# First norm of a two-layer transformer kernel: row sums on TensorE, four units tile by tile, bias tables moved

## The chip, the cores and the metric

The kernel runs on one core of one Trainium2 chip. The metric is device time in microseconds (us), the median of three runs. Engine names are those of the profile: PE is TensorE, DVE is VectorE, ACT is ScalarE, POOL is GpSimd, SP issues the DMAs.

## The reference

The kernel computes two hybrid transformer layers on x (512 positions by 1024). Each sublayer first normalizes: `adaln_pre(h, g, shift, scale) = rms_norm(h, g) * (1 + scale) + shift`, where shift and scale are products of `ada_w` (1024 by 9216 per layer) with `silu(c)`. The first sublayer is a gated feed-forward network:

```
def swiglu(h, w13, w2):
    a, b = jnp.split(h @ w13, 2, axis=-1)
    return (jax.nn.silu(a) * b) @ w2
```

Attention, short convolution, gated delta rule and mLSTM follow, then a second feed-forward sublayer. Everything is float32. Attention adds a bias that depends on the distance of two positions (`t5_table[t5_bucket(dist)]`); the kernel builds these bias tables once.

## The kernel before

Activations are kept transposed: tile k of 8 holds 128 of the 1024 channels for all 512 positions. Every float32 operand of the large products is split in a high part (an ACT copy to fp32r) and a low part (a DVE subtraction), and each product takes three fp32r matmuls: high by high, low by high, high by low. Each engine has a queue that runs in program order, and semaphores join them. All the work that the change touches lies in the first 100 us, in the first feed-forward sublayer of layer 0:

- **Start.** SP loads the constants, x, the condition `cond`, the tables of the bias, and 8 parts of `ada_first` of 1 MB each (L1117 to L1128), with the weights of units 0 and 1 between them. PE turns x into 8 banks (L3413), ACT copies them to `xT` (L1755) and squares them (L1761), PE sums the squares against ones (L3430). DVE makes the shift and scale: 16 dot products along rows of 1024 (`first`, L1985; `dots`, L1982), then one addition and one scaling for all 8 tiles (`prepare_start`, L2852). PE runs fillers (`warm`, L3674) until that is done.
- **Norm.** For each of two halves of the positions and each k, DVE writes `hf` (L2292), ACT the high part `hH` (L1527), DVE the low part `hL` (L2298).
- **Units.** A unit is 128 output columns of `w13`: 8 tiles, three matmuls each. Units 0 and 1 go half by half as `hL` comes, unit 2 behind them (`open_three`, L3461 to L3463); unit 3 runs last, whole (`products_third`, L3482 to L3484).
- **Bias tables.** PE forms distance rows by one-hot products (L3418 to L3421), ACT copies them out (L1770 to L1773), SP writes them to DRAM and reads them back skewed (`SKEW`, `CSKEW`, L1184, L1185). Between units 2 and 3 PE flips the skewed rows (L3440) and ACT copies them to `bm` (L1781). POOL copies `cb` out of `CSKEW` (L3305) once the last `hL` is written, and then makes four sums `tF` (L3324).
- **First pair.** After unit 3, `chunk` begins with `classical(f, 0)` (L3539 to L3541), 48 matmuls, whose weights come from `RW`: ACT splits the first 8 tiles (`group1`, L1357), DVE makes their low part (L2057). `pair_out` on DVE (L2176, L2178) needs ACT's Silu of unit 0 and its copy `pair_high` (L1458).

## Time and profile before

| what | us |
|---|---|
| median of three runs | 3389.28 (3389.25 to 3390.62) |
| the profiled execution | 3389.15 |
| its span in the profile | 3387.4 |
| first matmul of unit 0 | 44.11 |
| first matmul of the first pair | 70.48 |

The span covers the program's instructions; 1.75 us of the execution lie around it. Engine times in the trace are counted from the start of the span. Times of PE are modelled at their end, so that starts are compared.

### The profile page before, as it was taken

What the parts mean: (1) busy time and instruction counts of PE and PEld (TensorE: products, weight loads), DVE (VectorE), ACT (ScalarE), POOL (GpSimd) and SP (SyncE); (2) the same over time, 40 slices, a digit from 0 to 9 for tenths busy, and PEclk for the clock granted to TensorE, in tenths of its full rate; (3) what the DMA queues carried; (4) which work ended last, traced back from release to release, by engine and by line L of the source; (5) the groups of instructions that cost most, each with busy time, mean ns of one, the idle gap of its engine ahead of it and who ended that gap; (6) DMA issues with size and microseconds to landing.
All of it is one profiled execution on the core that took longest, in us unless ns stands there. A gap on an engine that the chain in (4) does not pass through costs nothing. (4 is left out here: it accounts for less than half of the span.)

```text
span 3387.4 us, 51035 instructions
## 1 busy us (share of the span) xinstructions
PE 3329.7 (98%) x19808; PEld 2811.7 (83%) x19808; DVE 2267.5 (67%) x3615; ACT 1317.6 (39%) x2095; POOL 438.0 (13%) x329
## 2 busy tenths in 40 slices
PE   8999999999999999999999999999999999999999
PEld 7989877788888898987778888886888888788887
DVE  6877757658775677785765877657666525766642
ACT  5424344535333433334453523243443324443321
POOL 2000200222000300020022200121200011120002
PEclk9999999999999999999999999999999999999999
DMA  6463523113542345442201353321233332223332
GB/s 252 148 229 129 166 86 94 32 39 127 176 145 96 112 154 211 144 150 88 87 26 54 128 192 124 101 77 52 81 99 99 105 102 63 68 82 94 96 104 85
DMA packets 88629, 380.90 MB, mean 112 GB/s; under 512 B 9774, under 2 KB 10926, under 8 KB 77192
## 3 DMA queue, kind: packets, MB, share of 16 engines
q1 hardware_dynamic: 88456, 378.52, 33.5%
q8 instruction: 117, 1.92, 0.2%
q14 instruction: 56, 0.46, 0.0%
HBM read 376.36 MB, written 2.12 MB: 112 GB/s over the span
## 5 line engine op out<-in xcount | busy, mean ns | idle before, releaser
L2001 DVE TENSOR_TENSOR wL<-wR,wH 128x1024 fp32r<-128x1024 f32 (+2 forms) x160 | 207.9, 1299 | 195.4 <-ACT wH L1289 195.2
L1289 ACT ACTIVATE wH<-wR 128x1024 fp32r<-128x1024 f32 (+2 forms) x158 | 175.0, 1107 | 381.3 <-PE bank L3452 305.6
L3697 PE MATMUL bank<-hH,wH 128*128 128x512 f32 x640 | 271.6, 424 | 0.0
L3566 PE MATMUL bank<-gHc,wH 128*128 128x512 f32 x660 | 256.8, 389 | 0.0
L3567 PE MATMUL bank<-gHc,wL 128*128 128x512 f32 x660 | 256.8, 389 | 0.0
L3568 PE MATMUL bank<-gLc,wH 128*128 128x512 f32 x660 | 256.7, 389 | 0.0
L3699 PE MATMUL bank<-hL,wH 128*128 128x512 f32 x640 | 251.6, 393 | 0.0
L3539 PE MATMUL bank<-hH,wH 128*128 128x512 f32 x640 | 249.7, 390 | 1.2 <-DVE wL L2057 1.2
L3698 PE MATMUL bank<-hH,wL 128*128 128x512 f32 x640 | 250.5, 391 | 0.0
L3540 PE MATMUL bank<-hH,wL 128*128 128x512 f32 x640 | 249.4, 390 | 0.0
L3541 PE MATMUL bank<-hL,wH 128*128 128x512 f32 x640 | 249.0, 389 | 0.0
L3450 PE MATMUL bank<-hH,wH 128*128 128x512 f32 x640 | 249.0, 389 | 0.0
L3451 PE MATMUL bank<-hH,wL 128*128 128x512 f32 x640 | 249.0, 389 | 0.0
L3452 PE MATMUL bank<-hL,wH 128*128 128x512 f32 x640 | 249.0, 389 | 0.0
L3149 DVE SCALAR_TENSOR_TENSOR xn<-bank,par,xn 128x511 f32<-128x511 f32 (+1 forms) x176 | 131.6, 747 | 120.3 <-ACT xn L1921 108.6
L1982 DVE CUSTOM_DVE_ANT_0 adaw<-adaw,cond 128x1024 f32<-128x1024 f32 x144 | 194.6, 1370 | 10.7 <-DMA adaw<-in_ada_w 10.3
L2057 DVE TENSOR_TENSOR wL<-RW,wH 128x512 fp32r<-128x512 f32 (+1 forms) x200 | 189.7, 977 | 15.1 <-ACT wH L1361 7.9
L3493 PE MATMUL bank<-tH,wH 128*128 128x256 f32 x640 | 181.1, 283 | 0.0
L3494 PE MATMUL bank<-tH,wL 128*128 128x256 f32 x640 | 181.1, 283 | 0.0
L3495 PE MATMUL bank<-tL,wH 128*128 128x256 f32 x640 | 181.1, 283 | 0.0
L1389 ACT ACTIVATE wH<-wR 128x1408 fp32r<-128x1408 f32 x52 | 71.8, 1381 | 261.7 <-PE bank L3568 261.7
L3697 PEld LDWEIGHTS bank<-hH,wH 128*128 128x128 f32 x640 | 121.0, 189 | 40.0 <-issue 19.6
(567 smaller groups left out, 8683.0 us busy)
## 6 DMA issues: line engine op xcount, KB each, us to landing
RW<-in_ffn_wq SPq DMA_DIRECT2D x80, 1024.0 KB, 5.6
adaw<-in_ada_w SPq DMA_DIRECT2D x144, 512.0 KB, 4.4
wR<-in_w_up SPq DMA_DIRECT2D x88, 512.0 KB, 3.6
wR<-in_ffn_w SPq DMA_DIRECT2D x56, 704.0 KB, 4.1
wR<-in_w_mix SPq DMA_DIRECT2D x72, 512.0 KB, 3.6
wR<-in_w_down SPq DMA_DIRECT2D x32, 704.0 KB, 4.1
wR<-in_w_in SPq DMA_DIRECT2D x40, 512.0 KB, 3.6
ada<-in_ada_first SPq DMA_DIRECT2D x8, 1024.0 KB, 12.1
```

The source lines that it names most:

```text
L3450: pe.matmul(o, wH[n][:, k, :], rH[:, r, :], start=start and k == 0, stop=False)
L3451: pe.matmul(o, wL[n][:, k, :], rH[:, r, :], start=False, stop=False)
L3452: mm = pe.matmul(o, wH[n][:, k, :], rL[:, r, :], start=False, stop=stop and k == tiles - 1)
L3539: pe.matmul(o, wh[:, k, :], hH[:, r, :], start=start and k == 0, stop=False)
L3540: pe.matmul(o, wl[:, k, :], hH[:, r, :], start=False, stop=False)
L3541: mm = pe.matmul(o, wh[:, k, :], hL[:, r, :], start=False, stop=not start and k == TT - 1)
L3566: pe.matmul(o, wh[:, k, :], gHc[:, k, c], start=k == 0, stop=False)
L3567: pe.matmul(o, wl[:, k, :], gHc[:, k, c], start=False, stop=False)
L3568: mm = pe.matmul(o, wh[:, k, :], gLc[:, k, c], start=False, stop=k == KH - 1)
L3697: pe.matmul(o, wH[n][:, k, :], hH[:, k, :], start=k == 0, stop=False)
L3698: pe.matmul(o, wL[n][:, k, :], hH[:, k, :], start=False, stop=False)
L3699: mm = pe.matmul(o, wH[n][:, k, :], hL[:, k, :], start=False, stop=k == KT - 1)
```

## The change

SP's order is new: `par` comes ahead of the parts, unit 3's load and the parts 5 to 7 follow by their waits, and the bias rows' write and the skewed reads stand behind the first pair's load and ahead of the second's. DVE moves four of the eight tiles of x and adds up the squares; PE sums them with one matmul instead of sixteen. For five of eight tiles the dot products go to PE: `part_sums` multiplies 8 row blocks, four at a time on 32 columns each, with the turned condition, ACT copies the sums, `part_columns` adds the four groups (a weight load of 128 columns for one output column). DVE keeps the last three as before. Shift, scale and norm then go tile by tile over all positions, and so do the four units (`first_four`). The fillers are gone. The bias rows are formed inside `first_four`, and the flips stand right ahead of the first pair, which waits for all four copies. `ada_first` is laid out by column for the five parts, on the host. Left out below: the tiles' places, semaphore names, the small helpers of ACT and DVE that the text names.

```diff
-ADA_PARTS = tuple((2 * c, 2 * c + 2) for c in range(KT))
+FIRST_TILES = (26, 30, 34, 38, 8, 12)
+FIRST_PE = 5
...
-        ada0 = [place(f"ada0{j}", [P, KT, D], at=at) for j, at in enumerate((o_g + 28 * TB, o_h))]
+        first_rows = [place(f"ada0{t}", [P, 2, D], at=o_g + t * TB) for t in FIRST_TILES]
+        ada0 = [first_rows[c] for c in (0, 1, 2, 3, 4, 0, 1, 5)]
...
+            sp.dma_start(par[:, 0:C_END1], a["par1"][0]).then_inc(S.par_in, 16)
...
-                ada_part(c)
-                if c < 2:
-                    sp.dma_start(wR[c][:, 0:KT, :], a["ffn1_w13"][0, c]).then_inc(S.w_in[c], 16)
+                if c in (5, 6):
...
+                if f == 0 and l == 0:
+                    for k in range(2):
+                        ada_part(k)
+                        sp.dma_start(wR[k][:, 0:KT, :], w13[l, k]).then_inc(S.w_in[k], 16)
+                    for k in range(2, 5):
+                        ada_part(k)
+                    unit(ubase + 2, w13[l, 2], KT, 0)
+                    ada_part(5)
+                    unit(ubase + 3, w13[l, 3], KT, 1)
+                    for k in range(6, KT):
+                        ada_part(k)
+                    sp.wait_ge(S.dc, 4)
...
+                    sp.wait_ge(S.dc, 4)
+                    pair(f, 0, wq, l)
                     sp.wait_ge(S.bias_sb, 1)
                     sp.dma_start(bias_dram, BROW[:, :]).then_inc(S.bias_out, 16)
                     sp.dma_start(cbias_dram, CROW[:, :]).then_inc(S.bias_out, 16)
-                unit(ubase + 2, w13[l, 2], KT, 0)
-                if start:
-                    sp.wait_ge(S.ada0_done, 4)
-                elif f:
-                    sp.wait_ge(S.c_o, at(S.c_o, TT))
-                pair(f, 0, wq, l)
-                unit(ubase + 3, w13[l, 3], KT, 1)
-                if start:
                     sp.wait_ge(S.bias_out, 32)
-                    sp.wait_ge(S.x_turned, KT)
+                    sp.wait_ge(S.dc, 5)
+                    sp.wait_ge(S.ada0_done, 2)
                     sp.dma_start(SKEW[:, :, :], bass.AP(bias_dram.tensor, 0, [[1, P], [640, H], [1, T]])).then_inc(S.skew_in, 16)
                     sp.dma_start(CSKEW[:, :, :], bass.AP(cbias_dram.tensor, 0, [[1, P], [1056, H], [1, 896]])).then_inc(S.skew_in, 16)
-                pair(f, 1, wq, l)
+                    pair(f, 1, wq, l)
...
-                gate_silu(0, 0)
-                pair_high(0)
                 if between:
                     between()
-                gate_silu(1, 2)
-                group1(f, 0)
-                single(f, 0, 2, 2)
-                sum_high(f, sub, 0)
-                pair_high(1)
-                act.wait_ge(S.w_used, at(S.w_used, ubase + 4))
-                single(f, 0, 3, 5)
-                if between:
+                    gate_silu(0, 0)
+                    group1(f, 0)
+                    pair_high(0)
+                    gate_silu(1, 2)
+                    act.wait_ge(S.w_used, at(S.w_used, ubase + 4))
+                    single(f, 0, 2, 2)
+                    single(f, 0, 3, 5)
+                    pair_high(1)
+                    sum_high(f, sub, 0)
                     act.wait_ge(S.cb_set, 1)
...
+            def first_norm():
+                for j in range(TT):
+                    k = 2 * j + 1
+                    act.wait_ge(S.x_turned, k + 1)
+                    act.activation(xT[:, k, :], bank[k][:, :], ACT.Copy).then_inc(S.x_copied, 1)
+                    first_square(2 * j)
+                    first_square(2 * j + 1)
+                act.wait_ge(S.ct, 1)
+                act.activation(CT[:, :, :], bank[4][:, 0:2 * P].rearrange("p (k c) -> p k c", k=KT), ACT.Copy).then_inc(S.ct, 1)
+                first_high(0)
+                first_sums(0)
+                first_high(1)
+                first_sums(1)
+                act.wait_ge(S.ms, 1)
+                act.activation(rstd[:, :], bank[MS_BANK[0]][:, :], ACT.Ln, bias=eps, scale=1.0 / D).then_inc(S.ln, 2)
+                logs[0] += 2
+                act.wait_ge(S.ln, 2)
+                act.activation(rstd[:, :], rstd[:, :], ACT.Exp, scale=-0.5).then_inc(S.rstd, 2)
+                first_sums(2)
+                for k in range(KT):
+                    for e, c in enumerate(HALVES):
+                        act.wait_ge(S.hf, 2 * k + e + 1)
+                        act.activation(hH[:, k, c], HB[e][k // TT][:, k % TT, :], ACT.Identity,
+                                       bias=mod[:, k:k + 1]).then_inc(S.h_hi, 1)
+                    if k == 0:
+                        first_sums(3)
+                        first_high(2)
+                    if k == 1:
+                        first_sums(4)
+                    if k == 2:
+                        first_high(3, fourth)
+                    if k == 3:
+                        first_bias()
...
+                def normed(k):
+                    if k == 0:
+                        dve.wait_ge(S.x_copied, TT)
+                        dve.wait_ge(S.rstd, 2)
+                    dve.wait_ge(S.mod0, 2 * k + 2)
+                    for e, c in enumerate(HALVES):
+                        dve.scalar_tensor_tensor(HB[e][k // TT][:, k % TT, :], xT[:, k, c], modA[:, k:k + 1], rstd[:, c],
+                                                 ALU.mult, ALU.mult).then_inc(S.hf, 1)
+                def normed_low(k):
+                    for e, c in enumerate(HALVES):
+                        dve.wait_ge(S.h_hi, 2 * k + e + 1)
+                        dve.scalar_tensor_tensor(hL[:, k, c], HB[e][k // TT][:, k % TT, :], mod[:, k:k + 1],
+                                                 hH[:, k, c].bitcast(F32), ALU.add, ALU.subtract).then_inc(S.h_lo, 1)
+                def part(c):
+                    if c >= FIRST_PE:
+                        first(c)
+                    shifted(c)
+                    scaled_by(c)
                 begin(0)
-                for c in range(KT - 1):
-                    first(c)
-                    if 0 < c < 3:
-                        lo_seam(0, c - 1)
+                for k in range(0, KT, 2):
+                    dve.wait_ge(S.x_turned, k + 1)
+                    dve.tensor_copy(xT[:, k, :], bank[k][:, :]).then_inc(S.x_moved, 1)
+                for k in range(1, KT):
+                    if k < KT - 1:
+                        dve.wait_ge(S.sq0, k + 1)
+                    else:
+                        dve.wait_ge(S.last_sq, 2)
+                    if k > 1:
+                        dve.wait_ge(S.sq_sum, k - 1)
+                    dve.tensor_tensor(squares[0], squares[0], squares[k], ALU.add).then_inc(S.sq_sum, 1)
                 dve.wait_ge(S.par_in, 16)
-                first(KT - 1)
-                dve.wait_ge(S.ada0_done, KT)
-                dve.tensor_tensor(mod[:, 0:2 * KT], mod[:, NMOD:NMOD + 2 * KT], col(C_ADAB, 2 * KT), ALU.add).then_inc(S.mod_set, 1)
-                dve.wait_ge(S.mod_set, at(S.mod_set, 1))
-                dve.scalar_tensor_tensor(modA[:, 0:KT], mod[:, KT:2 * KT], 1.0, col(C_NORM, KT), ALU.add,
-                                         ALU.mult).then_inc(S.mod_set, 1)
-                dve.wait_ge(S.mod_set, at(S.mod_set, 2))
+                low(0)
+                part(0)
+                low(1)
+                part(1)
+                normed(0)
+                normed(1)
+                for k in range(KT):
+                    normed_low(k)
+                    if k + 2 < KT:
+                        part(k + 2)
+                        normed(k + 2)
+                    if k in (1, 3):
+                        low(2 + k // 2)
+                dve.tensor_tensor(shd[:, :], mod[:, TT:KT], mod[:, 0:TT], ALU.subtract).then_inc(S.t_d, 1)
+                dve.sem_inc(S.mod_set, 2)
...
+                for r in range(2):
+                    for g in range(4):
+                        mm = pe.matmul(bank[DS_BANK[c % 2]][32 * g:32 * (g + 1), 0:2 * P], CT[:, 4 * r + g, :], rows[:, 4 * r + g, :],
+                                       start=r == 0, stop=r == 1)
+                mm.then_inc(S.ds, 1)
...
+            def part_columns(c):
+                if c == 0:
+                    pe.wait_ge(S.picks, 2)
+                if c >= 2:
+                    pe.wait_ge(S.mod0, 2 * c - 3)
+                pe.wait_ge(S.ds, 2 * c + 2)
+                for j in range(2):
+                    mm = pe.matmul(bank[DC_BANK[c % 2]][:, j:j + 1], DS[c % 2][:, j * P:(j + 1) * P], picks[:, :], start=True, stop=True)
+                mm.then_inc(S.dc, 1)
+            part_sums(0)
+            pe.wait_ge(S.sq_sum, KT - 1)
+            pe.matmul(bank[MS_BANK[0]][:, :], ones, squares[0], start=True, stop=True).then_inc(S.ms, 2)
+            part_columns(0)
+            part_sums(1)
+            part_columns(1)
+            part_sums(2)
...
+            def bias_rows():
+                pe.wait_ge(S.tab_in, 64)
+                pe.wait_ge(S.dc, FIRST_PE)
+                pe.wait_ge(S.mod0, 2 * FIRST_PE)
+                pe.matmul(bank[3][0:H, :], tab[:, :], OHR[:, 0:512], start=True, stop=True)
+                pe.matmul(bank[5][0:H, 256:384], tab[:, :], OHR[:, 512:640], start=True, stop=True)
+                for b, c, w, o in ((4, 0, 512, 0), (7, 512, 512, 0), (5, 1024, 32, 384)):
+                    mm = pe.matmul(bank[b][0:H, o:o + w], tab[:, :], OHF[:, c:c + w], start=True, stop=True)
+                mm.then_inc(S.bias_ps, 1)
...
+            def first_four():
...
+                pe.wait_ge(S.w_lo, 2)
+                for k in range(KT):
+                    pe.wait_ge(S.h_lo, 2 * k + 2)
+                    for u in range(2):
+                        part(u, k)
+                    if k < 3:
+                        part_columns(k + 2)
+                    if k < 2:
+                        part_sums(k + 3)
+                    if k == 2:
+                        bias_rows()
+                        pe.wait_ge(S.w_lo, 3)
+                        for r in range(2):
+                            part(2, r)
+                    if k >= 2:
+                        part(2, k)
+                    if k == 4:
+                        pe.wait_ge(S.w_lo, 4)
+                        pe.wait_ge(S.bias_sb, 1)
+                        for r in range(4):
+                            part(3, r)
+                for k in range(4, KT):
+                    part(3, k)
...
                 else:
+                    if between:
+                        between()
+                        pe.wait_ge(S.bm_set, H)
                     classical(f, 0)
...
-                open_three(ubase, n, late, not start)
-                if between:
-                    between()
-                pe.wait_ge(S.w_lo, at(S.w_lo, ubase + 4))
-                products_third(bank[3][:, :])
-                if between:
-                    pe.wait_ge(S.bm_set, H)
-                chunk(f, udn, 0, S.x_mid, KT * f)
+                if start:
+                    first_four()
+                else:
+                    open_three(ubase, n, late)
+                    pe.wait_ge(S.w_lo, at(S.w_lo, ubase + 4))
+                    products_third(bank[3][:, :])
+                chunk(f, udn, 0, S.x_mid, KT * f, None, between)
...
             def layer1(l):
-                if l == 0:
-                    warm(24)
-                    pe.wait_ge(S.mod_set, at(S.mod_set, 2))
-                    warm(3)
```

## Rows read from the trace of the kernel before

**Rows 1.** The page, part 1: busy time of each engine.

```profile
PE 3329.7 (98%) x19808; PEld 2811.7 (83%) x19808; DVE 2267.5 (67%) x3615; ACT 1317.6 (39%) x2095; POOL 438.0 (13%) x329
```

**Rows 2.** Busy time by stretch: PE, PEld, DVE, ACT, POOL, clock, DMA share, GB/s.

```profile
11.84:20.90 9.06, 8.23 (x38) 6.67 (x39) 4.49 (x7) 7.78 (x14) 0.00 (x0) 0.99 1.02 416
20.90:27.70 6.80, 6.80 (x16) 4.05 (x15) 6.55 (x11) 2.20 (x3) 0.00 (x0) 0.51 1.02 421
27.70:44.10 16.40, 16.40 (x77) 13.83 (x76) 16.02 (x35) 10.28 (x21) 0.00 (x0) 1.00 0.97 357
44.10:61.60 17.50, 17.50 (x147) 17.48 (x146) 10.57 (x21) 8.35 (x14) 7.28 (x33) 1.00 0.42 172
61.60:70.60 9.00, 9.00 (x35) 6.10 (x34) 6.39 (x5) 5.48 (x9) 8.90 (x3) 1.00 0.36 117
```

**Rows 3.** Timeline of PE: start us, us, operation; the four turning points.

```profile
44.11 0.47 PE L3461 MATMUL bank<-hH,wH 128*128 128x256 f32 x1
...
61.56 3.60 PE L3440 MATMUL bank<-skew,flip 128*128 128x512 f32 x8
...
70.48 0.39 PE L3539 MATMUL bank<-hH,wH 128*128 128x512 f32 x1
...
92.24 0.28 PE L3493 MATMUL bank<-hH,wH 128*128 128x256 f32 x1
```

**Rows 4.** Groups by shape, 0 to 56 us: count, busy us, mean ns, idle before.

```profile
L1982 DVE CUSTOM_DVE_ANT_0 ada<-ada,cond 128x1024 f32<-128x1024 f32 x16 | 18.7, 1221 | 15.9 <-DMA ada<-in_ada_first 15.8
...
L3674 PE MATMUL bank<-cst 128*128 128x256 f32 x54 | 11.8, 379 | 0.0
...
L1527 ACT ACTIVATE hH<-hf,mod 128x256 fp32r<-128x256 f32 x16 | 7.9, 505 | 8.7 <-DVE hf L2292 8.7
...
L2298 DVE SCALAR_TENSOR_TENSOR hL<-hf,mod,hH 128x256 fp32r<-128x256 f32 x16 | 7.7, 480 | 1.6 <-ACT hH L1527 1.6
...
L2292 DVE SCALAR_TENSOR_TENSOR hf<-xT,modA,rstd 128x256 f32<-128x256 f32 x16 | 7.5, 478 | 0.0
...
L3413 PE MATMUL bank<-cst,xin 128*128 128x128 f32 x32 | 6.4, 392 | 11.8 <-DMA cond<-in_c 11.8
...
L1755 ACT ACTIVATE xT<-bank 128x512 f32<-128x512 f32 x8 | 4.6, 596 | 1.3 <-PE bank L3413 1.3
...
L2237 DVE TENSOR_TENSOR wL<-wR,wH 128x1024 fp32r<-128x1024 f32 x3 | 3.7, 1220 | 0.0
...
L1308 ACT ACTIVATE wH<-wR 128x1024 fp32r<-128x1024 f32 x3 | 3.0, 1051 | 0.0
...
L1761 ACT ACTIVATE sqt<-xT 128x512 f32<-128x512 f32 x4 | 2.5, 632 | 1.6 <-PE bank L3430 1.6
```

**Rows 5.** Timeline of DVE: the first norm tile, two adds of one chain.

```profile
38.23 0.87 DVE L2292 SCALAR_TENSOR_TENSOR hf<-xT,modA,rstd 128x256 f32<-128x256 f32 x2
...
106.33 0.68 DVE L2052 TENSOR_TENSOR sum<-RW 128x512 f32<-128x512 f32 x1
...
107.05 0.69 DVE L2052 TENSOR_TENSOR sum<-sum,RW 128x512 f32<-128x512 f32 x1
```

**Rows 6.** Timeline of PE, a product on 32 columns, at 574 us.

```profile
574.72 0.45 PE L3874 MATMUL bank<-w2v,HID 128*32 128x64 f32 x16
```

**Rows 7.** DMA issues, 0 to 56 us: KB each, us to landing.

```profile
cskew<-bias_by_distance_up SPq DMA_DIRECT2D x1, 1792.0 KB, 13.7
```

**Rows 8.** Timeline of ACT, copies of the bias rows and Silu.

```profile
63.79 2.04 ACT L1781 ACTIVATE bm<-bank 128x512 f32<-128x512 f32 x4
...
65.70 0.62 ACT L1453 ACTIVATE sil<-bank 128x512 f32<-128x512 f32 x1
```

**Rows 9.** Timeline of DVE beside POOL, two splits.

```profile
59.67 2.95 DVE L2237 TENSOR_TENSOR wL<-wR,wH 128x1024 fp32r<-128x1024 f32 x1 [5.50 <-ACT wH L1308]
...
63.92 1.48 DVE L2178 TENSOR_TENSOR gLc<-gf,gHc 128x512 fp32r<-128x512 f32 x1 [0.70 <-ACT gHc L1458]
```

**Rows 10.** Timeline of POOL, same stretch.

```profile
61.62 6.04 POOL L3324 TENSOR_TENSOR tF<-hf,tF 128x1024 f32<-128x1024 f32 x2
```

204 lines of the change are left out of this document (138 added, 66 removed).

## The prediction

> **What bounds the kernel now.** I read the page first: PE is busy 98% of the span [rows 1], so time can only be won where PE does no useful work. The stretches [rows 2] and PE's timeline [rows 3] show that place. PE's first matmul of a unit starts at 44.11 us, everything before it is turning, squares and fillers, and from there PE has work without a break: 17.4 us of units 0 to 2 until 61.56, then flips and unit 3 until 70.48, then 96 matmuls of the first two pairs until 92.24, which is 21.76 / 96 = 0.227 us for one. So I compare one instant: the first matmul of the first pair, 70.48 before. Behind it the kernel is unchanged, and what that instant gains or loses the end gains or loses.
>
> What sets 44.11 is DVE. It makes 16 dot products of about 1.15 us (18.7 us busy, 15.9 idle for the DMA [rows 4]); the first norm tile follows at 38.23 [rows 5]. DMA moves 416 to 421 GB/s then [rows 2], so a part of 1 MB takes 2.5 us. After the change parts 5 to 7 and the weights of units 2 and 3 are asked for by progress; added up at that rate, the last part lands at about 38, long before DVE needs it at 57.
>
> **The start, step by step.** I take 0.05 us for each hop between engines.
> - x is turned from 11.84 to 18.2, 6.4 us [rows 4]. DVE moves its fourth tile by 18.2, then adds seven squares in one chain. A dependent add costs 107.05 - 106.33 = 0.72 [rows 5], so 7 x 0.73 = 5.1, over at 23.2. ACT's four copies and eight squares, 0.55 us each from start to start [rows 4], after a table load are over at 20.7, and hide below that chain.
> - PE turns the condition (20.6), ACT copies it (21.1), and `part_sums(0)` starts. It has 8 products of 256 columns, of two instructions each. A filler instruction of 256 columns costs 11.8 / 54 = 0.22 at the full clock [rows 4]: 16 x 0.22 = 3.5 if they run one by one, 0.9 if four run side by side. The row that bears on it is a product on 32 columns: 16 instructions of 64 columns in 0.45 us [rows 6], where 16 x 0.055 = 0.88 would be due in a row, and 0.2 of the 0.45 is the tail of the last. I take side by side.
> - The clock in this stretch was 0.51 before [rows 2], the 1.2 GHz level, after PE had turned x and multiplied narrow one-hot rows. After the change PE is emptier there, so I take half speed to 27.7: 1.8 us for each `part_sums`.
> - `part_sums(0)` ends at 22.9, the sum of squares starts at 23.3 and ends at 25.2, `part_columns(0)` at 26.1, `part_sums(1)` at 27.7. ACT takes the logarithm behind `first_sums(1)`, so at 28.1, and rstd is there at 29.5. DVE writes two norm tiles (4 x 0.40, from 0.87 for two less their overlap [rows 5]), then the low part of tile 0: 31.2 + 0.8 = 32.0. PE starts unit 0 at **32.1**, 12.0 us earlier than before.
>
> **The tiles, one after the other.** From here each tile needs a ring of engines. In the round of k = 0: PE's six matmuls 1.37, `part_columns(2)` 0.45, `part_sums(3)` 0.9, then ACT's copy 0.35, its weight split 1.0 [rows 4], two `hH` 0.9, and DVE's last `hL` 0.5 to 0.6: 5.6 us, in which PE works 2.7. ACT's copy `first_sums(3)` stands ahead of `hH` of tile 1 in its queue, and that closes the ring. The round of k = 1 loses the ACT split and gains DVE's low(2) of 1.14 (1.22 less overlap [rows 4]): 5.3. So k = 2 starts at 43.0. There the bias rows (1696 columns x 2 instructions at 0.22 per 256, 3.0 us) and unit 2's catching up make PE the bound, to 50.6 and 52.6. From k = 4 DVE is: per tile two dot products 2.3, shift and scale 0.4, norm 0.8, low 0.8 = 4.3 to 4.5 us, against PE's 9 matmuls of 2.05. Tile 7's last `hL` comes at 62.8. Tile 6 begins at 62.0, PE does tiles 6 and 7 of three units in 4.1 and half of unit 3 in 2.7: the four units end at **68.9**. The skewed reads wait for DVE's sixth tile (55.4) and for nothing later. Before, the second of them took 13.7 us to land among other loads [rows 7]; alone, 2.9 MB at 357 to 421 GB/s takes 7 to 8, so 63.7, five us ahead of need.
>
> **The end of the stretch.** Before, flips and ACT's split of the first pair's weights lay under unit 3. Now nothing lies under them. Flips: 8 instructions of 512 columns x 0.43 = 3.4, to 72.4. ACT's last copy to `bm` ends at 73.1 (four take 2.04, the last three of them under the flips [rows 8]). Only then come Silu 0.5 [rows 8], `group1` 1.0, `pair_high` 0.6, since ACT's queue puts them behind the tables: 75.1. DVE's low part of `g` stands ahead of the weights' low part in its queue: 0.6 and 1.14 alone. But POOL starts `cb` only at 63.8 (after tile 7 and the read) and its sums at 68.6, so that it is at work until about 80. Beside POOL the two kinds of DVE splits took 1.48 and 2.95 us [rows 9, 10], against 1.22 for the larger one alone [rows 4]. I take 1.3 and 2.3: the first pair starts at **78.7**, and PE has stood still for 6.3 us. What is queued behind it on PE is the whole kernel.
>
> **The sum.** 78.7 - 70.48 = 8.2 us later. Shares: the start is 12.0 earlier. From the first unit to the end of the fourth it is 36.8, where before it was 26.4 less 3.5 of flips, 22.9: 13.9 given back. The flips cost the same in both. The wait of 6.3 is new. -12.0 + 13.9 + 6.3 = 8.2. The clock adds to it: PE idles 6.3 us just ahead of dense work, and an idle spell may put the first products on the half clock. Between 0 and 3.4 us (half of the 6.8 us that the low stretch of [rows 2] lasted) I take 1.0. Forecast 3389.28 + 9.2 = **3398.5**; the profiled execution is at 3389.15, 0.13 below the median. Everything that I cost at nothing after 78.7 (splits of the second pair, `tF`, the DMA of the third) keeps its distance from the first pair, within 1 us, and the two pairs' 21.8 us of matmuls [rows 3] cover it.
>
> Bounds: full clock throughout gives 76.6, DVE splits untouched by POOL 77.1, both 75.0, so +4.5. At the low end DVE never waits after rstd: 32 norm steps of 0.40, six dot products of 1.15, two splits 2.5 and shifts 2.1 are 24.3 us, to 53.8; 4.5 of PE put the end of the units at 58.3, and flips and splits (3.5 + 0.7 + 0.5 + 1.0 + 0.6 + 0.6 + 1.15) the pair at 66.4, which is -4.1. At the high side, half clock until 44.7 gives 83.9, column products one by one 81.5, both 87: +13 to +17.
>
> Two rules of the skill speak here, and neither is in the sum. The Trainium skill ("TensorE: Matmul & The Clock Gate", section "Why this matters for your kernels") says that a spell without matmuls between two bursts sends the clock back to half. The trace has one such fall, at 0.51 [rows 2], but no idle spell of 6 us behind dense work; by the rule the clock term would be nearer 3.4 than 1, and the time 3400.9. The Trainium skill ("TensorEngine Tiling (Array Packing)", section "Key Properties") says that a change of tiling mode drains TensorE. Five `part_sums` switch twice each; a drain priced at the tail of a filler (0.38 - 0.22 = 0.16 [rows 4]) would make 1.6 us, and the time 3400.1. The one product on 32 columns [rows 6] shows no such price by itself.
>
> **Rivals.**
> - *The ring and the uncovered split both hold, as forecast* (chance 0.57): +7 to +14, by 77.3 to 84 for the first pair.
> - *The ring is looser* (0.30): full clock early, POOL out of the way, shorter hops. For it: the low clock before came after narrow products, and the split beside POOL is one row. Then +1 to +6.8, around 3393.
> - *DVE becomes the only bound, the other side* (0.04): ACT and PE keep ahead so that DVE never waits. It decides at the last `hL`: if that comes by 54 instead of 62.8, the first pair starts at 66.4, 4.1 us earlier: 3385.2. Against it: ACT's queue order, which makes DVE wait in both first rounds. For a gain of over 0.2% the pair would have to start by 63.7, 2.7 us under that floor, which nothing here gives.
> - *TensorE's part does not do what it says* (0.04): column products in a row on the half clock, a part of 3.5 to 7 us each, five times: first pair at 87, 3406.
>
> **How the numbers follow.** Within 0.2% (6.8 us, about what a measurement of this kernel can tell from no change) lie the looser ring and the other side: same 0.34. Slower is the forecast and the last rival: 0.61. The 0.05 left is for a gain that I do not see. The range reaches from 3388 (the looser ring's lower end) to 3406.
>
> **What would show it.** Right: first unit near 32; gaps of 2 to 3 us in PE between tiles, DVE waiting for PE's columns in the first rounds and never from tile 4 on; the last `hL` near 63; the flips near 69; a gap of about 6 us before `classical(f, 0)`, ended by DVE's low part of `RW`. Wrong: the first pair before 72, or flips that end while ACT already splits the pair's weights, or a wait for the skewed read.

## The result and the profile after

| | before | after |
| --- | --- | --- |
| median, us | 3389.95 (4 runs) | 3408.95 (4 runs, 3408.45 to 3414.27) |
| ratio | | 1.0059, interval 1.0041 to 1.0076 |
| profiled execution, its span | 3387.4 | 3406.6 (its time 3408.45) |
| first matmul of a unit | 44.11 | 33.11 |
| first matmul of the first pair | 70.48 | 85.06 |

The change makes the kernel 19.0 us slower. The forecast was 3398.5 with a range to 3406: the sign is right, the size is half of what came, and the result lies outside the range. (The runs of before beside it had a median of 3389.95, 0.67 above the one of the prediction. The four runs of the changed kernel lie 5.8 us apart, so differences of 1 or 2 us against its median say little.) The first pair starts 14.58 us later instead of 8.2; the rest comes behind it.

The page, part 1, answers to [rows 1]:

```profile
PE 3328.1 (98%) x19760; PEld 2801.7 (82%) x19760; DVE 2265.7 (67%) x3622; ACT 1318.5 (39%) x2097; POOL 437.3 (13%) x334
```

Busy time by stretch answers to [rows 2]; the columns are the same (time, then PE, PEld, DVE, ACT, POOL, granted clock, DMA share, GB/s):

```profile
11.84:22.80 10.96, 7.37 (x56) 6.36 (x55) 7.19 (x11) 10.70 (x19) 0.00 (x0) 1.00 1.02 421
22.80:36.50 13.70, 10.82 (x52) 6.58 (x52) 5.76 (x13) 3.16 (x7) 0.00 (x0) 0.50 1.00 400
36.50:57.00 20.50, 14.90 (x70) 9.33 (x71) 11.58 (x29) 7.94 (x20) 0.00 (x0) 0.75 0.19 69
57.00:76.97 19.97, 19.60 (x80) 14.71 (x79) 10.64 (x27) 5.23 (x10) 5.43 (x33) 1.00 0.56 199
76.97:85.05 8.08, 0.59 (x2) 0.03 (x1) 5.56 (x4) 4.45 (x8) 7.92 (x4) 0.74 0.37 130
85.05:109.70 24.65, 24.64 (x96) 20.14 (x97) 22.27 (x27) 12.22 (x20) 9.86 (x5) 0.88 0.29 92
```

Three things to see. The clock's low level (0.50) holds from 22.80 to 36.50, and 36.50 to 57.00 is half at the one level and half at the other (0.75); the forecast had it full from 27.7. From 57.00 on PE is full (19.60 of 19.97) at the upper level. Then it does nothing (0.59 of 8.08), and the 96 matmuls behind that take 24.65 us at 0.88, where before they took 21.76 [rows 3].

PE's timeline (start, duration, line, operation, in brackets the idle time and what ended it) answers to [rows 3]:

```profile
20.72 1.07 PE L3595 MATMUL bank<-ada,CT 128*32 128x256 f32 x16 [0.63 <-ACT CT L1834]
...
25.89 1.93 PE L3595 MATMUL bank<-ada,CT 128*32 128x256 f32 x16
...
33.11 0.77 PE L3679 MATMUL bank<-hH,wH 128*128 128x512 f32 x1 [1.91 <-DVE hL L2985]
...
35.81 0.83 PE L3607 MATMUL bank<-picks,DS 128*128 128x1 f32 x4
36.56 1.07 PE L3595 MATMUL bank<-ada,CT 128*32 128x256 f32 x16
40.40 0.79 PE L3679 MATMUL bank<-hH,wH 128*128 128x512 f32 x1 [2.77 <-DVE hL L2985]
...
47.01 0.79 PE L3679 MATMUL bank<-hH,wH 128*128 128x512 f32 x1 [2.29 <-DVE hL L2985]
...
52.04 2.23 PE L3626 MATMUL bank<-ohf,tab 33*4 33x512 f32 x6
54.20 0.79 PE L3679 MATMUL bank<-hH,wH 128*128 128x512 f32 x1
...
67.04 0.50 PE L3679 MATMUL bank<-hH,wH 128*128 128x512 f32 x1 [0.37 <-DVE hL L2985]
...
73.97 3.59 PE L3633 MATMUL bank<-skew,flip 128*128 128x512 f32 x8
85.06 0.76 PE L3768 MATMUL bank<-hH,wH 128*128 128x512 f32 x1 [7.49 <-DVE wL L2142]
```

The 16 instructions of one `part_sums` (L3595) take 1.07 us at the upper level and 1.93 at the lower: the four column groups do run side by side. The rounds are 40.40 - 33.11 = 7.29 us, then 6.61 and 7.19 (the last holds the bias rows). From 54.20 PE has 78 products until the flips at 73.97, with one short wait of 0.37 us, at 67.04, for DVE's last `hL`. Behind the flips comes the wait of 7.49 us. DVE's timeline in the first rounds and at the end answers to [rows 5, 9]:

```profile
36.67 0.16 DVE L2963 TENSOR_TENSOR mod<-bank,par 128x2 f32<-128x2 f32 x1 [3.71 <-PE bank L3607]
...
43.75 0.16 DVE L2963 TENSOR_TENSOR mod<-bank,par 128x2 f32<-128x2 f32 x1 [3.41 <-PE bank L3607]
...
50.46 0.16 DVE L2963 TENSOR_TENSOR mod<-bank,par 128x2 f32<-128x2 f32 x1 [3.51 <-PE bank L3607]
...
80.19 1.49 DVE L2263 TENSOR_TENSOR gLc<-gf,gHc 128x512 fp32r<-128x512 f32 x1 [0.77 <-ACT gHc L1484]
81.60 6.12 DVE L2142 TENSOR_TENSOR wL<-RW,wH 128x1024 fp32r<-128x1024 f32 x2
```

DVE waits for PE's columns 3.71, 3.41 and 3.51 us. At the end, `gLc` takes 1.49 us and the two splits of the first pair's weights 6.12 together. Beside them POOL, which answers to [rows 10]:

```profile
71.49 4.82 POOL L3462 COPY cb<-cskew 128x16 f32<-128x16 f32 x32 [70.12 <-DMA cskew<-bias_by_distance_up]
76.36 2.34 POOL L3481 TENSOR_TENSOR tF<-hf,hf 128x1024 f32<-128x1024 f32 x1
78.78 5.10 POOL L3481 TENSOR_TENSOR tF<-hf,tF 128x1024 f32<-128x1024 f32 x2
83.84 3.34 POOL L3481 TENSOR_TENSOR tF<-hf,hf 128x1024 f32<-128x1024 f32 x1
```

POOL waited for the skewed read until 71.49 and is at work until 87.2; in the kernel before it was through with its last `tF` at 71.0, so that the splits beside it (the two of the first pair's weights took 4.25 us, from 67.31) lay under the flips and unit 3, and those of the second pair came behind it.

### The profile page after: what moved, and what is told of

It reads as the page before. It is cut to its first block and busy times, and to the rows that moved or that the text cites. A ratio compares the mean times of both kernels' runs of the same rounds, so it can differ in the third digit from the quotient of the medians.

```text
span 3406.6 us, 50971 instructions
## 1 busy us (share of the span) xinstructions
PE 3328.1 (98%) x19760; PEld 2801.7 (82%) x19760; DVE 2265.7 (67%) x3622; ACT 1318.5 (39%) x2097; POOL 437.3 (13%) x334
```

## The experiments

Each experiment has a median of the kernel before measured beside it, 3388.65 to 3389.08; the gain or loss is against the changed kernel's 3408.95 unless it says otherwise. Since 3408.95 was measured beside a before of 3389.95, every such gain may be about 1 us too large; the ratios don't have that fault. The low stretches of the clock are told in us from the start of the span, as the trace of each kernel's profiled execution has them. The first four experiments take one suspect each.

**The split ahead of the copies.** ACT's queue gets the first pair's split before the four copies to `bm`:

```diff
                 if between:
-                    between()
                     gate_silu(0, 0)
                     group1(f, 0)
                     pair_high(0)
+                    between()
```

> ACT makes group1 and the high part of the first pair's weights ahead of its four copies to bm, instead of behind them. Theory A (the end of the stretch is a chain behind the flips: bm copies, Silu, group1, pair_high, then DVE's two low parts, and the half clock in the first pair is the price of PE standing still for 8.1 us): Silu starts at about 68, DVE's low parts are over by about 77, while the flips still run; the first pair starts at 78 to 79.5 instead of 85.05, the half clock in it is gone (2.9 us more), and the time is 8 to 10 us below that of the changed kernel, 3399 to 3401. Rival B (POOL's work is what DVE and the pair wait for, or another wait takes the place): pair start not before 82, and the time above 3404. Rival C (the half clock comes whatever PE did just before): pair start 78 to 79.5, but 96 matmuls of the first pair still take 24.7 us, time 3402 to 3403.

Measured: 3405.89, ratio to before 1.0049 [1.0035, 1.0063]. The pair starts at 78.45 as expected, but only 2 to 3 us of the 6.6 are kept. PE's timeline shows where the others went:

```profile
78.45 0.50 PE L3768 MATMUL bank<-hH,wH 128*128 128x512 f32 x1 [0.69 <-ACT bm L1864]
...
93.77 0.50 PE L3768 MATMUL bank<-hH,wH 128*128 128x512 f32 x1 [4.12 <-DVE wL L2142]
```

DVE's timeline of the same kernel says why:

```profile
83.62 2.88 DVE L2142 TENSOR_TENSOR wL<-RW,wH 128x512 fp32r<-128x512 f32 x1
86.43 3.44 DVE L2117 TENSOR_TENSOR tL<-tF,tH 128x1024 fp32r<-128x1024 f32 x1
```

PE now waits 4.12 us ahead of the second pair, for DVE. Two splits that take 0.69 and 1.22 us when DVE works alone take 2.88 and 3.44 beside POOL's block sums (77.9 to 88.8 here). Theory A has the start of the pair right and its price wrong; the time is that of rival B, another wait in the place of the old one, though B had the pair late as well.

**POOL later.** POOL starts its block sums only behind DVE's split of the first pair:

```diff
                 if between:
                     between()
+                    pool.wait_ge(S.q_lo, of(S.q_lo, f, 4, 3, 1))
                 block_sum(0, h12, h11)
```

> POOL starts its block sums only after DVE has made the low part of the first pair's weights. If DVE's split is slow because POOL works beside it (its first half took 3.3 us from 81.6 where the like takes 1.2 alone), the pair starts at about 83, 2 us earlier than 85.05, unless the compressed bias on POOL ran beside it instead. If POOL has nothing to do with it, the pair starts at 85.0 and the split takes as long as before.

Measured: 3417.00 (one run). Its ring ran slower (half clock until 45.3 and again until 62.3), so the flips start at 77.05, 3.08 us later than in the changed kernel, and only what follows them can be compared, on PE's timeline:

```profile
77.05 3.59 PE L3634 MATMUL bank<-skew,flip 128*128 128x512 f32 x8
85.19 0.76 PE L3769 MATMUL bank<-hH,wH 128*128 128x512 f32 x1 [4.54 <-DVE wL L2142]
...
104.80 0.80 PE L3769 MATMUL bank<-hH,wH 128*128 128x512 f32 x1 [6.35 <-DVE wL L2142]
```

and on DVE's:

```profile
83.27 0.69 DVE L2263 TENSOR_TENSOR gLc<-gf,gHc 128x512 fp32r<-128x512 f32 x1 [0.77 <-ACT gHc L1484]
83.88 1.82 DVE L2142 TENSOR_TENSOR wL<-RW,wH 128x1024 fp32r<-128x1024 f32 x2
```

With POOL idle `gLc` takes 0.69 us and the two splits 1.82 together, instead of 1.49 and 6.12, and PE's wait ahead of the pair is 4.54 us instead of 7.49. From the start of the flips to the pair it is 8.14 us instead of 11.09: POOL beside DVE costs the first pair 2.95 us. The bill comes at the second pair, which waits 6.35 for DVE's low parts behind POOL's late sums.

**Fillers in the ring.** PE multiplies fillers where it stood still, behind the column sums:

```diff
+            def fill(count, b):
+                for _ in range(count):
+                    pe.matmul(bank[b][:, 0:2 * P], ident, cst[:, 0:2 * P], start=True, stop=True)
             part_sums(0)
+            fill(4, 3)
...
             part_sums(1)
+            fill(2, 3)
             part_columns(1)
             part_sums(2)
+            fill(5, 3)
...
                     if k < 2:
                         part_sums(k + 3)
+                        fill(6 - k, 6)
```

> Fillers of 256 columns stand in PE's idle spells after the column sums of parts 0 to 2 and in the rounds of tiles 0 to 6 (some 40 in all). Clock theory (PE's half clock from 22.8 to 36.5 and its returns at 39.9, 46.7, 53.5 come from PE standing still, and cost the ring some 4 us): the granted clock stays at its upper level from 23 to 55, the rounds of tiles 0 and 1 shrink from 7.29 and 6.6 us to 5.5 to 6.2, the last unit's end comes 2 to 4 us earlier, and the first pair at 81 to 83. Rival (the rounds are set by ACT's and DVE's work and hops; the clock costs nothing, and a filler that is under way only delays the products): rounds of 7 us or more and the pair at 85 or later.

Measured: 3400.97, ratio 1.0038 [1.0024, 1.0051], 8.0 us faster than the changed kernel although PE does more. Busy time by stretch:

```profile
15.00:37.70 22.70, 19.37 (x142) 14.08 (x140) 13.75 (x28) 12.85 (x25) 0.00 (x0) 0.92 1.01 400
37.70:48.50 10.80, 10.26 (x57) 6.28 (x56) 6.47 (x17) 3.11 (x8) 0.00 (x0) 1.00 0.31 106
```

PE's timeline at the end of the stretch:

```profile
68.62 3.59 PE L3641 MATMUL bank<-skew,flip 128*128 128x512 f32 x8
79.69 0.77 PE L3777 MATMUL bank<-hH,wH 128*128 128x512 f32 x1 [7.47 <-DVE wL L2142]
```

The clock is 0.92 and 1.00 where it was 0.50 to 0.75; the rounds are 5.8 and 5.3 us, the flips start at 68.62 instead of 73.97. So 5.35 us of the 14.58 go with the low clock in the ring. The wait ahead of the pair is as long as in the changed kernel, 7.47.

How far PE's standing still is the cause can be read from the low stretches. In the changed kernel they are 22.8 to 36.5, 39.9 to 43.3, 46.7 to 50.1 and 53.5 to 57.0; the second and the third begin inside PE's waits of 2.77 and 2.29 us. With the fillers the first is 21.3 to 24.7 and these two are gone. The last one stays, at 48.6 to 52.0, just past the stretch shown above, and PE hadn't stood still for it: it begins at the end of the narrow bias rows, which had run without a break from 45.64, with 0.54 us of idle time ahead of them. Whether the bias rows bring it is not shown: in three kernels further down (compressed bias left out, ring opened, all four) they pass without it.

**Column sums twice.** 32 instructions instead of 16 for each part:

```diff
-                for r in range(2):
+                for r in (0, 1, 0, 1):
```

> Every column sum of a part is made twice over (32 instructions instead of 16, the same result). By the ring theory the column sums of parts 3 and 4 lie on the path of rounds 0 and 1, and those of parts 0 and 1 on the path to the norm: each adds 0.7 us at the upper clock level and 1.3 at the lower, so the first unit starts about 1.5 to 2.5 us later, rounds 0 and 1 are 1 us longer, and the pair starts 2.5 to 4 us later, at 87.5 to 89. If the instructions of one part did not run side by side but something else hid them, or DVE is the only bound, the pair moves by under 1 us.

Measured: 3403.38 (one run), 5.6 us faster, pair at 82.97. My expectation had the sign wrong: the doubled work lies on the path (1.56 us from first to last instruction at the upper level, 0.69 for the single ones), but it also fills PE, and the low stretches shrink from 13.7 us at the start to 3.4. In the trace the low level holds for 17.1 us of the first 100 instead of 34.1. The clock outweighs the work; this is the fillers' result from another side. Of the gain 3.2 us are there when PE leaves the first two pairs; the rest comes later, so 5.6 is not the price of the clock in the ring alone.

**The tables alone.** The kernel before, its first norm untouched, with the flips behind unit 3 and ACT's queue as in the changed kernel:

```diff
                 open_three(ubase, n, late, not start)
-                if between:
-                    between()
                 pe.wait_ge(S.w_lo, at(S.w_lo, ubase + 4))
                 products_third(bank[3][:, :])
                 if between:
+                    between()
                     pe.wait_ge(S.bm_set, H)
```

> The kernel before, with its old first norm; only the tables are moved: PE's flips stand behind unit 3, ahead of the first pair, and ACT's queue has the order of the changed kernel (four copies to bm, Silu, group1, pair_high). Theory A (the move of the tables is a cost of its own, flips with nothing under them and then a chain of splits): unit 3 is over at 67.0, the flips at 70.4, the last copy to bm at 71.3, pair_high at 73.3, DVE's two low parts by 75.5 if POOL leaves them alone and by 78 if not; the first pair starts 5 to 7.5 us later than 70.48, with up to 3 us more of half clock: 3394 to 3399, about half of the 19 us. Rival B (nearly all of the loss is in the ring of the first norm): the first pair starts under 3 us later, 3390 to 3392.

Measured: 3394.03 (11 runs, 3392.86 to 3398.94), ratio 1.0015 [1.0006, 1.0024], beside 3389.08. PE's timeline:

```profile
62.59 0.50 PE L3491 MATMUL bank<-hH,wH 128*128 128x512 f32 x1 [1.05 <-DVE wL L2246]
...
68.17 3.59 PE L3449 MATMUL bank<-skew,flip 128*128 128x512 f32 x8
76.31 0.77 PE L3548 MATMUL bank<-hH,wH 128*128 128x512 f32 x1 [4.55 <-DVE wL L2066]
```

The first pair is 5.83 us late, of which 1.05 is a new wait for unit 3's low part that the flips used to cover, and 4.55 the chain behind the flips, with POOL idle for it (DVE's `gLc` 0.69, both splits 1.82). Theory A came out, at the low end of its range: the move of the tables alone costs 5 us of the 19. The profiled execution is the slowest of the eleven, 4.9 us above their median, with half clock from 75.1 to 82.0 in the first pair, so the trace shows where the time goes and the median how much it is.

The changed kernel doesn't have the wait of 1.05. Without it, 4.78 for the move, 5.35 for the clock and 2.95 for POOL make 13.08 of 14.58. If the shares add, which no run shows, 1.5 us are left for the new first norm even without its low clock: what its early start wins, its rounds more than give back.

**Fillers and split together, and POOL's order.** The fillers with the split, and then also POOL's sums ahead of the compressed bias:

```diff
                 if between:
-                    between()
+                    pool.wait_ge(S.bias_out, 32)
                 block_sum(0, h12, h11)
...
                 block_sum(2, h22, h12)
+                if between:
+                    between()
```

> The fillers in the ring and ACT's split ahead of the copies to bm, both. The fillers alone brought the end of the fourth unit from 73.9 to 68.6; the split alone brought the first pair from 85.05 to 78.4, but then the second pair waited 4.5 us for DVE, whose low parts of the block sums come behind POOL. Theory A (the two add up, and POOL, which can't start before the skewed read of the compressed table has landed, is the next bound): pair start 72.8 to 74, second pair waiting 3 to 5 us, time 3396 to 3398.5. Theory B (POOL's chain moves with the read, the second pair doesn't wait): 3392 to 3394. Theory C (they overlap: the time is that of the fillers alone): 3400 to 3402.

> As the fillers and the split together, and POOL makes its four block sums ahead of the compressed bias, as soon as the tables are written out, instead of behind the skewed read. If POOL's late start (71.5 in the changed kernel, 54.2 before) is what holds the second pair, its wait of 3 to 5 us goes: pair start 72.8 to 74, no gap before the second pair, time 3391 to 3393.5. If the wait was DVE's or ACT's own work, the time stays within 1 us of the run without this edit. If POOL beside DVE's last norm tiles slows these, the fourth unit ends after 69.5 and the gain is under 2 us.

Measured: 3401.16, ratio 1.0035 [1.0021, 1.0049], and 3402.83, 1.0040 [1.0027, 1.0054]. Both start the first pair at 72.9, and both lose it again: the second pair waits 4.08 and 7.11 us. For the first one the time is that of theory C, but the pair's start and the wait are those of theory A: the two edits do add up at the first pair, and 5.2 of the 6.7 us won there against the fillers alone are gone again when PE leaves the two pairs. The second one's edit was a miss, by a detail that I had not followed: POOL's fourth sum waits for the flips, so the compressed bias came only behind that, and ACT's queue waits for it. POOL's timeline:

```profile
72.32 2.40 POOL L3481 TENSOR_TENSOR tF<-hf,hf 128x1024 f32<-128x1024 f32 x1 [2.15 <-PE bank L3643]
74.66 7.32 POOL L3462 COPY cb<-cskew 128x16 f32<-128x16 f32 x32
```

ACT's, where the bracket names the wait:

```profile
82.01 1.71 ACT L1368 ACTIVATE tH<-tF,mod 128x256 fp32r<-128x256 f32 x4 [4.53 <-POOL cb L3462]
```

**Without the compressed bias.** To tell POOL's lateness from the queues of DVE and ACT, POOL fills `cb` with zeros in the kernel with fillers and split. This kernel leaves the compressed bias out, so it serves for its times only:

```diff
-                for n in range(32):
-                    c = 31 - n
-                    mm = pool.tensor_copy(cb[:, :, :, n], sk[:, c:c + 8 * TT - 7:8, :, 0])
+                mm = pool.memset(cb[:, :, :, :], 0.0)
```

> Fillers and split first, and POOL's 32 copies of the compressed bias replaced by one fill with zeros, so that the compressed bias is left out and POOL's four block sums start some 5.5 us earlier (66.5 instead of 72.4). If POOL's lateness is what the second pair pays (DVE's splits ran beside POOL and took twice their time alone, four of them 5 us too long, and the second pair waited 4.4 us): the wait is under 1 us, the second pair starts at 84 to 85 instead of 88.2, and the time is 3 to 4 us below 3401.2. If DVE's or ACT's own queue sets it: no change within 1 us.

Measured: 3395.41, ratio 1.0022 [1.0013, 1.0031], 5.8 us below the run with it, although its flips start 1.3 us later. (Ten runs from 3393.29 to 3399.33; the profiled one is 2.8 above their median.) The second pair doesn't wait at all: from 74.26 on the 96 matmuls run through, and PE waits for DVE only behind them, 1.24 us. So what the second pair paid for is POOL's 32 copies, which make the block sums late, and not DVE's or ACT's own queue. In the first 100 us of this kernel's trace the low level holds from 20.1 to 26.9 alone, and PE's timeline has this wait ahead of the last tile:

```profile
62.98 0.50 PE L3685 MATMUL bank<-hH,wH 128*128 128x512 f32 x1 [1.66 <-DVE hL L2985]
```

Here PE waits 1.66 us for DVE's last `hL`, where with the same ring and the low stretch behind the bias rows it waits 0.35 (fillers alone).

**Fillers behind the flips.** 28 in the changed kernel, and 14 in the one with fillers in the ring; the edit shown is the second:

```diff
                         pe.wait_ge(S.bm_set, H)
+                        for _ in range(14):
+                            pe.matmul(bank[7][:, 0:2 * P], ident, cst[:, 0:2 * P], start=True, stop=True)
```

> The changed kernel with 28 fillers of 256 columns (some 6 us) behind the flips, in the 8.1 us in which PE stands still; nothing else moves. If the half clock in the first pair (80.8 to 91.1) is the price of that standing still, it goes, and the 96 matmuls of the first pairs take 21.8 us instead of 24.7: pair start 85 and 3405.5 to 3406.5. If the clock falls for another reason, both stay, at 3408 to 3410.

> Fillers in the ring and 14 of them behind the flips too. A filler is two instructions of 0.21 us (the 28 of the run before took 12 us, not the 6 that I had reckoned, and delayed the pair by themselves), so these take 5.9 us and end before the pair is ready. If PE's standing still before the first pair is what brings the half clock of 75.9 to 82.7, it goes: pair start 79.7 as without them, 96 matmuls in 21.8 us instead of about 23.5, time 3399 to 3399.5 instead of 3401. Rival: half clock stays, or the pair moves, 3401 or more.

Measured: 3412.74, 1.0066 [1.0051, 1.0082], and 3400.22, 1.0035 [1.0022, 1.0048]. The 28 took 12 us and pushed the pair to 93.3, so that time says nothing, though its trace has no low stretch in the pairs. The 14 fit. Busy time over the 96 matmuls:

```profile
79.60:101.30 21.70, 21.70 (x96) 17.92 (x96) 20.85 (x25) 12.07 (x20) 9.91 (x5) 1.00 0.27 97
```

PE's timeline ahead of them:

```profile
72.81 6.31 PE L3821 MATMUL bank<-cst 128*128 128x256 f32 x28 [0.69 <-ACT bm L1864]
79.57 0.50 PE L3777 MATMUL bank<-hH,wH 128*128 128x512 f32 x1 [0.45 <-DVE wL L2142]
```

The clock is full and the 96 matmuls take the 21.7 us of the kernel before, so the low clock in the first pair is the price of PE standing still before it. The other traces agree: ahead of the first or the second pair nine kernels have waits of 4 us or more, ten in all, and each time a low stretch begins inside the wait or within 1.0 us behind it; behind none of the waits there of 0.73 us or less does one begin. What it costs in the end these runs can't tell: 0.75 us against the kernel without these 14, with runs that spread over 4.4 us. PE waits 0.92 us for DVE behind the pairs, which returns part of the gain.

**The ring opened.** On the kernel with fillers, PE makes columns and sums ahead of the tile:

```diff
                 for k in range(KT):
+                    if k < 3:
+                        part_columns(k + 2)
+                    if k < 2:
+                        part_sums(k + 3)
+                        fill(1, 6)
                     pe.wait_ge(S.h_lo, 2 * k + 2)
                     for u in range(2):
                         part(u, k)
-                    if k < 3:
-                        part_columns(k + 2)
-                    if k < 2:
-                        part_sums(k + 3)
-                        fill(6 - k, 6)
```

(and `fill(1, 3)` for `fill(5, 3)` ahead of the first tile).

> The kernel with fillers in the ring, in which PE now makes the columns of part k+2 and the column sums of part k+3 ahead of tile k's products instead of behind them (and three fillers instead of sixteen between the first tiles, since little idle time should be left). Ring theory (a round is one chain: PE's products, columns and sums, ACT's copy, its split and hH, DVE's hL, all in a row because PE's queue puts the columns behind the tile): DVE no longer waits for the columns, rounds 0 and 1 shrink from 5.8 and 5.3 us to 3 to 3.6, DVE's two dot products of a tile are the bound from tile 5 on, the last hL comes at 57 to 58.5 instead of 62.4, the fourth unit ends at 61.5 to 64.5 instead of 68.6, and the first pair starts at 72.5 to 75.5 instead of 79.7: 3394 to 3397. Rival (PE or DVE has no room left, the rounds only look like a chain): rounds above 5 us, pair at 79 or later, 3400 or more.

Measured: 3393.34 (11 runs, 3392.63 to 3395.76), ratio 1.0014 [1.0005, 1.0024], 7.6 us below the kernel with fillers alone. PE's timeline:

```profile
62.34 3.59 PE L3641 MATMUL bank<-skew,flip 128*128 128x512 f32 x8
73.31 0.77 PE L3777 MATMUL bank<-hH,wH 128*128 128x512 f32 x1 [7.37 <-DVE wL L2142]
```

Rounds 0 and 1 take 3.4 and 2.2 us, the flips start 6.28 us earlier, and DVE's waits for PE's columns in the rounds are gone. So the ring was closed by the place of columns and sums in PE's queue, and moving them opens it. The low stretch behind the bias rows is absent here, but that can't be the gain: with the fillers alone PE had to wait for DVE's last `hL` all the same.

**All four.** Fillers, open ring, split ahead of the copies, and POOL with three sums, the compressed bias, then the fourth.

> All together: fillers, columns ahead of the tiles, ACT's split ahead of the copies to bm, and POOL's first three block sums ahead of the compressed bias, the fourth behind it. If the four causes (clock, ring, chain behind the flips, POOL's lateness) are the whole loss, the fourth unit ends at 62 to 64.5, the first pair starts at 66.5 to 69 (before the change: 70.48), the second pair waits under 2 us, and the time is 3386 to 3390, below the changed kernel by 19 to 23 us and about equal to or up to 3 us below the kernel before. If POOL beside DVE only shifts (the compressed bias now runs beside the second pair's splits): a wait of 3 to 5 us stays and the time is 3390 to 3393.

Measured: 3388.87 (11 runs, 3387.09 to 3389.19; the profiled one is the fastest), ratio to before 0.9999 [0.9990, 1.0008]. PE's timeline:

```profile
61.89 3.59 PE L3642 MATMUL bank<-skew,flip 128*128 128x512 f32 x8
66.17 0.50 PE L3778 MATMUL bank<-hH,wH 128*128 128x512 f32 x1 [0.69 <-ACT bm L1864]
...
78.08 0.50 PE L3778 MATMUL bank<-hH,wH 128*128 128x512 f32 x1 [0.73 <-DVE wL L2142]
...
90.51 0.38 PE L3732 MATMUL bank<-hH,wH 128*128 128x256 f32 x1 [1.26 <-DVE wL L2142]
```

The pair starts at 66.17, 4.31 us earlier than in the kernel before, and of these PE gives back 0.73 and 1.26 in front of the second pair and of what follows, both waits for DVE's low parts. The four edits bring back as much as the change lost, and this version is even with the kernel before, not better. Smaller differences drown: far behind the stretch single low stretches come and go from execution to execution (1659 to 1663 in the trace of before, 568 to 571 in this one), each worth up to 1.7 us. The four edits don't size each other's shares: the open ring goes past what the changed kernel lost there, and pays for the flips that nothing covers.

## Why the prediction was wrong

The direction held, and the ring and the uncovered split are there as forecast. Three terms of the sum were mis-sized: the clock, POOL's effect, and what comes behind the pair's start. In the terms of the prediction, -12.0 + 13.9 + 6.3 for the pair's start became -11.0 + 18.0 + 7.5, then 2.9 instead of 1.0 for the clock in the pairs, and 1.5 instead of nothing behind them.

- **The start.** Forecast 32.1, measured 33.11; `part_sums` side by side, as taken from [rows 6]. ACT's copy of the third part stands ahead of `hH` of tile 0 in its queue, which the sum had left out, and it waited for `part_sums(2)` at the low level (1.93 us instead of 1.07):

```profile
31.27 0.39 ACT L1814 ACTIVATE DS<-bank 128x256 f32<-128x256 f32 x1 [1.69 <-PE bank L3595]
```

With the fillers that part runs at the upper level, and the first unit starts at 32.03.
- **The clock in the ring** is the step that failed. I had the low level end at 27.7, because it had in the kernel before [rows 2], and the sum's only later clock term was 1.0 us in the first pair. But before, fillers stood in PE's queue there [rows 4], and the change takes them out. The level stayed low until 36.5 and came back three times: 5.35 us at the flips, by what the fillers give back, and that covers the 5.1 us by which the flips came later than forecast (73.97 against 68.9). With the fillers in, the ring's own numbers hold to the last step: rounds of 5.8 and 5.3 (forecast 5.6 and 5.3), k = 2 at 43.1 (43.0), last `hL` over at 62.4 (62.8), flips at 68.62 (68.9). The bound that I worked out for this, half clock until 44.7 (83.9), was near the truth, and I gave it no case of its own.
- **DVE the bound from tile 4.** True for the time of the flips, and only just: in the changed kernel as with the fillers PE waits once for DVE, at the last `hL`, 0.37 and 0.35 us. DVE's own chain was as forecast, and PE was nearly as late, because half clock lay on its products behind the bias rows, which the forecast didn't have. Where that stretch is absent (compressed bias left out), PE waits 1.66 us at the same place. So the flips within 0.3 us of the forecast, with the fillers, are DVE's chain; it was luck that PE's unforeseen half clock cost nothing on top.
- **The end of the stretch.** Flips 3.59 (3.4). The wait was 7.49 instead of 6.3: `gLc` 1.49 (1.3), and the split until the pair could start about 3.4 (2.3). The forecast had POOL beside DVE's splits too, but priced them between the rows alone and the rows beside; they came at the full price, and above the 2.95 of [rows 9]. The effect was priced at 1.6 us and measured 2.95. POOL began at 71.49, not 63.8: the read was issued at 61.0, not at 55.4, since DVE's sixth tile was late through the ring, and took some 10 us, not 8.
- **The clock in the first pair.** 1.0 us taken, 2.9 measured (24.65 against 21.76), near the 3.4 that the sum had as its end.
- **Everything behind 78.7 "keeps its distance".** False: 4.4 us were lost between the first pair's start (14.58) and the end (19.0). 2.9 is the clock; the other 1.5 were lost behind 109.7. The traces of before and after, laid side by side, show 1.25 of them in one place: at 264.97 PE waits 1.20 us for DVE's low part, since DVE had waited 1.79 us for the load of `RW` (0.54 in the kernel before). What made that load late is open.
- **The rule of the clock.** The Trainium skill ("TensorE: Matmul & The Clock Gate", section "Why this matters for your kernels") says that idle spells between bursts send the clock back to half. The runs agree in the main: half clock from 22.8 to 36.5, while PE's idle spells were 0.5 to 1.9 us, and again behind idle spells of 2.77 and 2.29 us; with fillers the first ends at 24.7 and the two returns are gone. The stretch behind the bias rows has no such idle spell ahead of it, so the rule doesn't cover it. I had applied it to the last wait only. The Trainium skill ("TensorEngine Tiling (Array Packing)", section "Key Properties") says that a change of tiling mode drains TensorE; such a drain hardly shows. Inside a part the 16 instructions take 1.07 us with tail, no more than a quarter of 16 x 0.22 and the tail. At the change of mode behind it, in the kernel with fillers, the first filler starts 0.31 us behind the last group of four (27.19 and 27.50), where group follows group at 0.22 to 0.24: about 0.1 us at most, against the 0.16 that the prediction took for a drain.
- **Rivals.** The looser ring lost to the clock; the other side asked for a ring that doesn't wait for ACT, and the open ring shows that this takes another order in PE's queue. The column products in a row did not come.

## What to carry to other kernels

When an engine's busy work is taken away, ask what else that work did: fillers and spare products can hold TensorE's clock, and in a chain of small steps with TensorE idle in between its products can come at double price (1.93 against 1.07 us for one `part_sums` here). Before a helper's result is moved ahead of a consumer, look at what the producer has queued in front of it: here one line's place in PE's queue was worth 6 us. And a late start on a side engine is not free because that engine isn't the bound; ask which burst on another engine it will meet.

## What the runs showed of the hardware that I had not expected

- DVE's `TENSOR_TENSOR` splits of fp32 tiles depend on what POOL does: 128x512 took 0.69 us alone and 1.4 to 2.9 beside POOL's block sums, 128x1024 1.22 alone and 3.4 beside; the scalar form of four 128x256 pieces 1.67 alone, 3.7 to 6.9 beside. POOL's 32 copies slowed in turn, 4.82 us alone and 6.3 to 7.4 beside DVE. Not every operation on DVE slows: `gf<-bank,sil`, 128x512 with one operand in `bank`, took 0.68 us in the midst of POOL's sums too (at 80.79 with the split ahead of the copies, POOL 80.40 to 85.96).
- More work can be less time: column sums made twice (one run) brought the end 5.6 us forward, with half as much time at the low level.
- Four products on 32 columns each, of 256 columns of fp32, run side by side: 16 instructions in 0.69 us from first start to last at 2.4 GHz and 1.30 at 1.2.
- The low stretches do not come alike in each execution: two kernels whose ring was that of the changed one (POOL later, fillers behind the flips) had them from 21.4 to 45.3 and 48.7 to 62.4, and their flips started at 77.05 instead of 73.97. One profile of a kernel whose PE is half idle carries an error of that size, and so do the 5.35 us above, which compare one profile with one.
